# Decay and rate LoRA products of an RWKV-7 scan: projected inputs read in place by half-height products instead of through a zero-padded copy

## What is computed

```python
lw = lw.reshape(bn, t, N_DIR, LORA_W)   # 2 directions x 64
la = la.reshape(bn, t, N_DIR, LORA_A)   # 2 directions x 64
wl = p['w0'] + jnp.einsum('btdr,drc->btdc', jnp.tanh(lw), p['w2'])
decay = jnp.exp(-jnp.exp(-jax.nn.softplus(-wl) - 0.5))
a = jax.nn.sigmoid(p['a0'] + jnp.einsum('btdr,drc->btdc', la, p['a2']))
kd = kf[:, :, None, :] * (1.0 + (a - 1.0) * p['k_a'])
def step(s, inp):                       # once forward, once reversed
    r_t, w_t, k_t, v_t, kk_t, a_t = inp
    sa = jnp.einsum('bhvk,bhk->bhv', s, kk_t)
    s = (s * w_t[:, :, None, :] - sa[..., None] * (kk_t * a_t)[:, :, None, :]
         + v_t[..., None] * k_t[:, :, None, :])
    return s, jnp.einsum('bhvk,bhk->bhv', s, r_t)
```

## Time and profile before

| | us |
|---|---|
| median of 3 runs (lowest, highest) | 1237.46 (1235.92, 1238.48) |
| the profiled execution's own time | 1235.28 |
| span of its instructions | 1233.6 |
| PE busy | 1126.9 (91%) |
| DVE busy | 683.0 (55%) |
| ACT busy | 394.3 (32%) |
| POOL busy | 373.8 (30%) |
| L961, MATMUL busy, 2 x 144 instructions | 21.7 + 19.5 |
| L1138, ACT busy, 72 copies | 18.2 |
| L1302, DVE busy, 36 additions | 24.9 |

### The profile page before, as it was taken

How to read it: one execution, slowest core, us unless ns; L and a number is a source line. 1 busy time by engine, 2 the same in 40 slices (tenths; PEclk the granted TensorE clock), 3 DMA queues, 4 the chain that set the end, 5 groups by cost and what they waited for, 6 DMA issues and landing times. The chain is left out here.

```text
span 1233.6 us, 36488 instructions
## 1 busy us (share of the span) xinstructions
PE 1126.9 (91%) x16691; PEld 1009.9 (82%) x16691; DVE 683.0 (55%) x937; ACT 394.3 (32%) x706; POOL 373.8 (30%) x326
## 2 busy tenths in 40 slices
PE   4869998999889999995899999999999999869997
PEld 0369887899869988975899999999999999646686
DVE  0561004948746222255677777778787877374542
ACT  3331100101113233223354344444434443253321
POOL 6161111111303222313333334334534444041110
PEclk9979998999989999997899999999999999979999
DMA  9501233211102201000000000000000000180121
GB/s 375 174 1 35 69 108 107 69 35 44 60 1 73 79 29 35 1 1 10 3 4 13 4 3 4 4 4 3 4 4 4 4 3 4 63 315 35 69 103 52
DMA packets 29974, 61.76 MB, mean 50 GB/s; under 512 B 3296, under 2 KB 21364, under 8 KB 28666
## 3 DMA queue, kind: packets, MB, share of 16 engines
q1 hardware_dynamic: 28332, 54.17, 12.7%
q10 hardware_dynamic: 1488, 5.24, 1.1%
HBM read 49.68 MB, written 9.73 MB: 48 GB/s over the span
## 5 line engine op out<-in xcount | busy, mean ns | idle before, releaser
L609 PE MATMUL ps<-input_rounded,weights_rounded 128*128 128x386 f32 x768 | 266.3, 347 | 10.2 <-DVE zc L779 5.2
L611 PE MATMUL ps<-input_rounded,weights_rest 128*128 128x386 f32 x768 | 262.2, 341 | 0.0
L610 PE MATMUL ps<-input_rest,weights_rounded 128*128 128x386 f32 x768 | 262.2, 341 | 0.0
L1261 POOL TENSOR_TENSOR arena<-arena,lvl 128x512 f32<-128x512 f32 x108 | 136.3, 1275 | 206.9 <-DVE arena L1340 105.9
L609 PEld LDWEIGHTS ps<-input_rounded,weights_rounded 128*128 128x128 f32 x768 | 147.0, 191 | 18.4 <-issue 12.6
L610 PEld LDWEIGHTS ps<-input_rest,weights_rounded 128*128 128x128 f32 x768 | 146.8, 191 | 0.9 <-issue 0.6
L611 PEld LDWEIGHTS ps<-input_rounded,weights_rest 128*128 128x128 f32 x768 | 146.9, 191 | 0.0
L412 POOL TENSOR_TENSOR weights_rest<-arena,weights_rounded 128x2048 fp32r<-128x2048 f32 x16 | 75.6, 4722 | 209.8 <-ACT weights_rounded L458 209.8
L1014 PE MATMUL ps<-arena 64*64 64x64 f32 x2880 | 103.2, 221 | 17.6 <-DVE arena L1358 16.4
L1014 PEld LDWEIGHTS ps<-arena 64*64 64x64 f32 x2880 | 94.0, 137 | 20.7 <-DVE arena L1358 20.7
L1006 PE MATMUL ps<-arena 64*64 64x64 f32 x2880 | 104.1, 221 | 6.2 <-issue 3.4
(11 more groups left out here) (227 smaller groups left out, 1958.4 us busy)
## 6 DMA issues: line engine op xcount, KB each, us to landing
arena<-in_w_in SPq DMA_DIRECT2D x16, 1024.0 KB, 5.4
arena<-in_ada_w SPq DMA_DIRECT2D x12, 1024.0 KB, 6.8
mix_scratch<-zc SPq DMA_DIRECT2D x4, 1158.0 KB, 9.2
out<-arena SPq DMA_DIRECT2D x9, 512.0 KB, 2.6
zc<-in_x_sample ACTq DMA_DIRECT2D x2, 2048.0 KB, 20.5
zc<-in_w_out SPq DMA_DIRECT2D x4, 1024.0 KB, 8.4
arena<-in_x_sample SPq DMA_DIRECT2D x8, 512.0 KB, 3.3
zc<-mix_scratch SPq DMA_DIRECT2D x1, 2316.0 KB, 18.2
```

What stands on the lines that cost most here:

```text
L609: pe.matmul(o, w_hi[:, k, cut], hi_of_h[:, k, cols_b], start=(k == 0), stop=False)
L610: pe.matmul(o, w_hi[:, k, cut], lo_of_h[k][:, cols_b], start=False, stop=False)
L611: last = pe.matmul(o, w_lo[:, k, cut], hi_of_h[:, k, cols_b], start=False, stop=(k == KT - 1))
L1261: pool.tensor_tensor(flat(Um[l % 3]), TA[n % 2][:, :, :, 0, :].rearrange("p d a c -> p (d a) c"), lvl[:, l, :].unsqueeze(1).to_broadcast([ ...
```

## The change

`lora` makes one product per direction, `which` and head pair, with 64 rows of weights (`w[r, ...]`, the half of direction `d`) and 64 columns read straight from `lwT` or `laT`: 16 products of 64 x 128 weights and 64 columns in place of 8 of 128 x 128 and 128 columns. Direction `d` is now collected in bank `4 + d` (decay and rate side by side), so the products of the two halves go to different banks. `ls`, its clearing and `stage_lora` go. There is one semaphore increment at the end of all 16 products, and one count `q_x` for both bias additions, which now go by direction: each writes half of `xw` and half of `av`, the two tiles being neighbours in `xa2`. Both `decay_tanh` and `rate_tanh` wait for both additions.

```diff
             def _(pe):
-                def lora(n, which):
-                    if which == 0:
-                        earlier(pe, q_mT, 2 * n)
-                    else:
-                        earlier(pe, q_v, n)
-                    pe.wait_ge(q_stage, 4 * n + 2 * which + 2)
-                    w = (w2s, a2s)[which]
-                    for a in range(PAIRS):
-                        last = pe.matmul(ps[:, 4 + which, P * a:P * a + P], w[:, P * a:P * a + P], ls[:, which, :],
-                                         start=True, stop=True)
+                def lora(n):
+                    earlier(pe, q_mT, 2 * n)
+                    earlier(pe, q_v, n)
+                    for which, (w, src) in enumerate(((w2s, lwT), (a2s, laT))):
+                        for a in range(PAIRS):
+                            for d, r in enumerate(HALVES):
+                                at = C * (PAIRS * which + a)
+                                last = pe.matmul(ps[:, 4 + d, at:at + C], w[r, P * a:P * a + P],
+                                                 src[r, STARTS[n][d]:STARTS[n][d] + C], start=True, stop=True)
                     last.then_inc(q_lora, 1)
...
-                        lora(na, 0)
-                        lora(na, 1)
+                        lora(na)
...
-                def stage_lora(n):
-                    earlier(act, q_lora, 2 * n)
-                    for which, src in enumerate((lwT, laT)):
-                        for d, r in enumerate(HALVES):
-                            act.activation(ls[r, which, r], src[r, STARTS[n][d]:STARTS[n][d] + C], ACT.Copy).then_inc(q_stage, 1)
-
                 def decay_tanh(n):
-                    act.wait_ge(q_xw, n + 1)
+                    act.wait_ge(q_x, 2 * (n + 1))
                     act.activation(xw, xw, ACT.Tanh, scale=0.5).then_inc(q_tw, 1)
...
                 def rate_tanh(n):
-                    act.wait_ge(q_xa, n + 1)
+                    act.wait_ge(q_x, 2 * (n + 1))
...
-                        stage_lora(na)
                         decay_tanh(na)
                         rate_tanh(na)
...
-                for v in (ls, S[0], keep):
+                for v in (S[0], keep):
...
-                def add_bias(n, which):
-                    dve.wait_ge(q_lora, 2 * n + which + 1)
-                    dve.tensor_tensor((xw, av)[which], by_direction(4 + which), wide(("w0", "a0")[which]),
-                                      ALU.add).then_inc((q_xw, q_xa)[which], 1)
+                def add_biases(n):
+                    dve.wait_ge(q_lora, n + 1)
+                    earlier(dve, q_bN, n)
+                    for d in DIRS:
+                        dve.tensor_tensor(both[:, :, d], ps[:, 4 + d, :].rearrange("p (k a c) -> p k a c", k=2, a=PAIRS),
+                                          biases[:, :, d, :].unsqueeze(3).to_broadcast([P, 2, PAIRS, C]), ALU.add).then_inc(q_x, 1)
```

More of the change, by code:

```diff
@@ L839, in hybrid_step_kernel @@
         q_ns = sem2("new_state_stored")
-        q_stage = sem2("lora_input_staged")
         q_lora = sem2("lora_multiplied")
-        q_xw = sem2("decay_bias_added")
-        q_xa = sem2("rate_bias_added")
+        q_x = sem2("gate_bias_added")
         q_tw = sem2("decay_tanh_ready")
@@ L891, in hybrid_step_kernel @@
         take = carve()
-        ls = take(2, P)
-        xw, av, LA, LB, kd = (take(2, PAIRS, C) for _ in range(5))
+        xa2 = take(2, 2 * PAIRS * C)
+        xw, av = (xa2[:, k].rearrange("p (d a c) -> p d a c", d=2, a=PAIRS) for k in range(2))
+        LA, LB, kd = (take(2, PAIRS, C) for _ in range(3))
         eA, eB, eN = LA, LB, xw
@@ L1293, in _ @@
             def _(dve):
[L1294 to L1298, removed]
-                def add_bias(n, which):
-                    dve.wait_ge(q_lora, 2 * n + which + 1)
-                    dve.tensor_tensor((xw, av)[which], by_direction(4 + which), wide(("w0", "a0")[which]),
-                                      ALU.add).then_inc((q_xw, q_xa)[which], 1)
+                biases = vec[:, VEC_ROWS["w0"][0]:VEC_ROWS["a0"][0] + VEC_ROWS["a0"][1]].rearrange("p (k d a) -> p k d a", k=2, d=2)
+                both = xa2.rearrange("p k (d a c) -> p k d a c", d=2, a=PAIRS)
+                def add_biases(n):
[4 more added lines that the diff above has]
+                                          biases[:, :, d, :].unsqueeze(3).to_broadcast([P, 2, PAIRS, C]), ALU.add).then_inc(q_x, 1)
                 def sum_decays(n):
@@ L1394, in _ @@
                     if A:
-                        add_bias(na, 0)
-                        add_bias(na, 1)
+                        add_biases(na)
                     if L:
```

## The result

The changed kernel takes 1255.38 us in the median of 4 runs (1254.62 to 1257.14); the kernel before 1237.97 in 4 runs. The ratio is 1.0142, 95% interval 1.0122 to 1.0163: slower by 15 to 20 us. Forecast were 1254 us and +17.1; the medians differ by 17.4.

What follows compares the result with a forecast made beforehand. PE was taken to bound the scan, so only its own work and added waits count. Burst 0, staging 0, and waits 0.8 + 1.4 + 14.9 = +17.1 us gave a forecast of 1254 us, range 1240 to 1287.

Steps and rivals of the forecast that it cites:

- The wait behind the burst: Steps 2 to 17: late tanh delays ACT's copy of Y, so PE's level-2 update waits 0.93 us each, 14.9 us.
- g: Moment when the LoRA burst ends on PE, 802.77 in step 9 before; other moments are given relative to it.
- The burst: LoRA products on PE: 128-column weight loads set the pace, 1.96 us against 1.98, taken as unchanged.
- short-burst rival: LoRA burst on PE: loads cost less than 0.11 us, bound 1.13 us, net +2.6, 1240 us; chance 0.11.
- rival of halves taking turns: LoRA burst on PE: the halves' loads go one after another, burst 3.7 us, net +49, 1287 us; chance 0.15.
- The staging: Four staging copies on ACT, 1.09 us, steps 1 to 17: hidden, so removing them gains 0.
- The first steps: Step 0: earlier burst start but later tanh, +0.8 us; step 1: nothing covers the wait for Y's copy, +1.4.
- clock rival: PE in the scan: a second idle stretch brings the low clock into other steps, ten blocks +9, 1264 us; chance 0.06.
- The sum: Whole kernel: 0.8 + 1.4 + 14.9 = +17.1 us, all three of them waits.

Runs made afterwards that it cites:

- by-gate version: Changed kernel, but decay and rate products counted separately in separate banks, each addition waiting for its own eight products, decay's tanh for the first addition only: 1234.38 us, ratio 0.9978.
- copy first: Changed kernel with ACT's copy of Y for level 1 moved ahead of the two gate operations: 1238.70 us, ratio 1.0016.
- split version: By-gate version with the decay's products moved between the level-1 product and update, the rate's behind that update, DVE's order likewise: 1223.48 us, ratio 0.9886.
- joint wait: Kernel before with only waits changed: both bias additions wait for all eight products, decay's tanh for both additions: 1259.67 us, ratio 1.0182.
- half weights: Changed kernel with weights of 64 instead of 128 columns in each product of the burst: 1238.47 us, ratio 1.0002.
- quadrant version: By-gate version with each 64 x 128 weight product cut into two of 64 x 64, one for each half of the output partitions: 1219.57 us, ratio 0.9850.

## Why the prediction was right, point by point

**The wait behind the burst, 16 x 0.93 = 14.9.** Right in place, cause and nearly in size. Tanh came 1.44 us after the burst (said: 1.43), the copy of `Y` at g + 3.73 (said: 3.73), the update at g + 3.88 (said: 3.78). The 0.1 us between is the one part that I took too small: I gave 0.05 us from the end of ACT's copy to PE's start, but it is 0.15 (816.56 to 816.71). The update stands 1.03 us later behind the burst than before, and steps grew by 1.01: 16.1 us in steps 2 to 17 instead of 14.9. That it is this wait is shown from both sides: alone it makes the kernel before slow, and without it (by-gate version) or without the copy standing behind it (copy first) the changed kernel isn't.

**The burst, 0.** Right: 1.94 us (said: 1.96). The loads of 128 columns set the pace: the burst followed the weight columns and not the moving ones. The rule in "TensorE: Matmul & The Clock Gate" of the Trainium skill, LDWEIGHTS, by which a load goes by its columns, agrees with 1.94, 1.90 and 1.03 us. The rows that I named for a load of 128 columns give 0.11 us (0.30 - 0.188); the 0.107 beside it was the estimate by that page's formula, and the sum used 0.11. The speed of up to twofold that "TensorEngine Tiling (Array Packing)" of the Trainium skill, Theoretical Speedup, gives for 64 rows was not there with 128-column weights, and came when columns were tiled as well (1.1 us). My short-burst rival rested on the 0.06 us of the small transposes, which don't carry over. The rival of halves taking turns was wrong for this order of instructions, and a third right for the order half after half.

**The staging, 0.** Right, shown by putting it back.

**The first steps, +0.8 and +1.4.** Step 0 gave 1.17 us by starting earlier and lost 1.60, net +0.4 instead of +0.8. Step 1 lost 2.55 instead of 1.4. The wait itself was right: the level-2 update started 5.81 us after the start of the burst instead of 4.36, so 1.45 later (PE waited 2.73 us for the copy of `Y` instead of 1.23). The other 1.1 us arise behind this update, where PE's waits are the same ones and equal to 0.01 us. There the same products ran for longer at the low one of the two levels (1.2 GHz), where a block of 32 matmuls took 1.97 us instead of 1.15: some 10 us before and some 14 after, an estimate from the mean clocks of 0.80 and 0.74 below. The stretches from the burst to the update and from the update to the next burst, first of the kernel before, then of the changed one (columns: us, busy of PE, loads, DVE, ACT, POOL, clock):

```profile
581.49:585.85 4.36, 3.13 (x53) 2.90 (x49) 3.29 (x5) 2.41 (x5) 1.14 (x1) 1.00 0.00 0
585.85:611.05 25.20, 20.42 (x480) 19.44 (x481) 15.08 (x25) 9.23 (x22) 10.76 (x12) 0.80 0.01 3
```

```profile
581.92:587.73 5.81, 3.08 (x69) 2.90 (x65) 3.72 (x5) 2.41 (x5) 1.27 (x1) 1.00 0.00 0
587.73:614.02 26.29, 21.52 (x480) 20.49 (x480) 13.80 (x25) 8.33 (x18) 10.42 (x11) 0.74 0.01 3
```

So the clock rival has a part in this one step, of about 1.1 us, a term that my sum did not have. The by-gate version, which starts the update as early as the kernel before, had 0.83 over the whole step like it and took 29.60 us. In the steady steps this rival was wrong for the changed kernel, their clock stayed at 1.00 from 640 to 1000 us.

**The sum** came to 19.1 in the two profiles against 17.1, and 17.4 between the medians. The errors (steady steps +1.2, step 1 +1.15, step 0 -0.4) are all small beside the one term that decides. That the forecast of the sum meets the medians to 0.3 us is closer than its terms are, and so partly luck.

## What to carry to other kernels

A merged wait costs what stands behind it in its queue, not what it guards: when two waits become one, take the later release, walk down the waiting engine's order to the first result that the bounding engine needs, and compare the delay with that result's slack (here 1.5 us against 0.6). Work freed from an engine that isn't the bound was worth nothing here by itself; what it allowed was to start the bounding engine's work in a gap of its own. Filler for such a gap must not come from a place where it already covers a latency. And cutting a float32 product into two of half height, side by side, saved nothing while the columns of the single weight load set the pace; cutting the columns as well did.

## What the runs showed of the hardware that was not expected

**DVE waits for POOL where both read from SBUF.** The scan lasts 1.22 us in all steps of the changed kernel and in step 0 of the kernel before, and 1.80 in the other steps of before. The row of its line in the kernel before (ns, min/median/max):

```profile
L1308 DVE TENSOR_TENSOR_SCAN arena<-arena x18: 1224/1796/1801, 562.4 to 1020.0; 128x512 f32<-128x512 f32 x18
```

POOL in step 9 of before:

```profile
804.01 1.28 POOL L1261 TENSOR_TENSOR arena<-arena,lvl 128x512 f32<-128x512 f32 x1 [3.73 <-PE ps L1006]
```

Before, POOL's multiplication ended at 805.29 and the scan had started at 804.57, 0.72 us of overlap, for 0.57 us more. After, it started at 814.07 and ended at 815.35, before the scan's start at 815.59. In the by-gate and the split version, whose tanh is early as before, the scan lasts 1.80 us in steps 1 to 17; with the late tanh (joint wait, copy first, half weights) 1.22. Other overlaps give the same loss, always 0.14 to 0.15 us less than the overlap: 0.58 us in steps 2, 9 and 14 of the version with half the moving columns gave scans of 1.66, and 0.67 us in the quadrant version gave 1.76. The row of the former:

```profile
L1297 DVE TENSOR_TENSOR_SCAN arena<-arena x18: 1224/1225/1662, 564.7 to 1042.1; 128x512 f32<-128x512 f32 x18
```

It is not only the scan. The decay of the state, two inputs in SBUF too, takes 1.76 us in the steady steps of both kernels, with 1.21 us of overlap, and 0.68 at the least; the factor (L1358), with one input in SBUF and one in the PSUM, keeps its 0.69 us even when POOL works beside it all the time (798.97 in step 9). "SBUF — State Buffer" in the Trainium skill says just this: a DVE instruction with two SBUF inputs contends with a GpSimd instruction that reads SBUF, and the one that starts second is blocked until the first has finished; the 0.14 us are not in it. In the scan's place the loss was hidden both ways, but it spoiled one expectation by exactly this amount.

**Four quadrants work side by side.** 64 matmuls of 64 x 64 weights and 64 columns on all four quadrants took 1.1 us, where 32 on the diagonal take 0.95. No product of the scan before used the quadrants off the diagonal.

**Changes of weight width cost about 0.1 us each.** From the start of the level-1 update to the start of a burst of 128-column weights are 1.08 us (799.71 to 800.79); to the start of the burst of 64-column weights at the same place are 0.98 (803.78 to 804.76). The split burst has one more change in and one more out: its two parts and what they take to leave are 1.03 and 1.04 us, together 0.13 more than the 1.94 of the whole burst, and the block ahead of its first part again takes 1.08 us.
